# Prompt attention of a hybrid decoder layer: weighted values for two heads side by side with the values as the stationary operand, rows scaled before they are transposed, the causal term as a product

## The chip, the cores and the metric

The kernel runs on one core of a Trainium2 chip. The metric is the device time of one launch in microseconds (us); lower is better. Work on the core is spread over TensorE (PE for its matrix products, PEld for the loading of the stationary operand), VectorE (DVE), ScalarE (ACT), GpSimd (POOL) and SyncE (SP, which issues the transfers here). PE writes into eight PSUM banks of 128 partitions by 512 fp32 columns; DVE and ACT read these. A product of two fp32 operands is recorded as two passes, each with its own weight load; a transpose is recorded as one.

## What is computed

One layer of a decoder for a prompt (512 tokens) and eight short samples. The change touches one piece of it, the attention of the prompt over itself: 8 heads, keys 96 wide, values 64 wide, four blocks of 128 queries, softmax over the keys up to the query's own position.

```python
MLA_HEADS, MLA_V, SEQ, Q_BLOCK = 8, 64, 512, 128

def mla_scores(qn, qp, kn, kp):
    s = jnp.einsum('bthd,bshd->bhts', qn, kn) + jnp.einsum('bthd,bsd->bhts', qp, kp)
    return s.astype(jnp.float32) * MLA_SCALE

def mla_prompt_attention(qn, qp, kn, kp, v):
    ...
    def block(args):
        i, qn_i, qp_i = args
        s = mla_scores(qn_i, qp_i, kn, kp)
        qpos = i * qb + jnp.arange(qb)
        s = jnp.where(kpos[None, :] <= qpos[:, None], s, -jnp.inf)
        p = jax.nn.softmax(s, axis=-1).astype(v.dtype)
        return jnp.einsum('bhts,bshd->bthd', p, v)
    o = lax.map(block, (jnp.arange(nb), qn_b, qp_b))
    return o.swapaxes(0, 1).reshape(B, T, MLA_HEADS, MLA_V)
```

Its result, transposed, is one half of the input of the layer's output projection. Everything else of the layer (projections, a gated linear attention, the samples' attention over a paged cache, cross-attention, a squared-ReLU MLP) is the same in both kernels.

## The kernel before

The program is written as one instruction stream for each engine; the order on an engine is the order of the code, and engines meet only through semaphores. Phases end with `meet`, where every engine waits for the others. The prompt's attention lies between `meet(·, 2)` and `meet(·, 3)`. Its inputs are in SBUF by then: `qT` and `kT` (96 partitions, a head's queries and keys in columns), `vp` (values, tokens on partitions, 64 columns for each head).

The phase walks 32 steps `n`, one for each block of queries `t` (0 to 3) and head `h` (0 to 7). A step of block `t` looks at `t + 1` blocks of 128 keys, so its scores are 128 to 512 columns wide. For one step:

- PE, line 918: scores of 128 queries by (t+1)·128 keys, contraction over 96, into one of three banks (0, 1, 2 in turn).
- DVE, line 1874: adds the `causal` block (0 or a large negative number) to the last 128 columns, in the bank; line 1875: the negated maximum of each row.
- ACT, line 1419: exponential with that maximum as bias into `pr` (three buffers), and the row's sum into `stat`.
- PE, line 925: t+1 transposes of 128 by 128 of `pr` into bank 3 or 6.
- DVE (even steps, line 1881) or ACT (odd steps, line 1427): copy of these to `prT` (two buffers).
- PE, line 934: weighted values, t+1 products with a 128-column block of `prT` as the stationary operand and 64 columns of `vp` as the moving one, into columns 64h to 64h+64 of bank 4 or 5 (`po`). Queries are on partitions.

Once in a block, behind its eighth head: DVE takes reciprocals of the eight sums (line 1888) and scales all of `po` into `ot` (line 1891), PE transposes `ot` (line 911, four transposes) into bank 7, and ACT copies that to `mixT` (line 1433). The lag between the engines is written into the loops: PE's iteration `n` does the scores of step n, the transposes of step n-2 and the values of step n-3; ACT's iteration `n` does the exponential of step n and then, for odd n, the copy of step n-2.

`make_plan` gives each use of a bank its number; `full` waits for a bank's filling, `reopen` for its release. `link` makes an engine wait for its own last instruction. During the phase SP loads the pages of the first sample, and POOL prepares weights of the phase behind it.

## Time and profile before

| | |
|---|---|
| median of 3 runs | 1341.59 us (1338.92 to 1341.65) |
| the profiled execution | 1340.34 us, its span 1338.5 us |
| PE busy | 1265.8 us (95%), 7851 passes |
| PEld busy | 1085.6 us (81%) |
| DVE, ACT, POOL busy | 606.1, 380.6, 258.2 us |
| the prompt's attention | 339.5 to 404.5 us of the span |

The page divides the span into 40 slices and gives each engine's busy share in tenths; a row for the granted clock of TensorE stands below it. A matrix pass is recorded with its whole latency, so passes that follow each other overlap in the record, and PE can show as busy while it works at far less than its rate. How fast the passes really follow each other is read from their merged rows: n passes in a row take (n - 1) intervals and one latency. Idle time of PEld and PE in front of an instruction, with the engine that ended it, tells where PE truly stood.

### The profile page before, as it was taken

The numbers are of one execution on the slowest core, as the hardware profiler recorded it, in microseconds if no ns is written. First come the engines' busy times: TensorE is split into PE (matmuls) and PEld (weight loads), VectorE is DVE, ScalarE is ACT, GpSimd is POOL, SyncE is SP. The second block draws the span as 40 slices with busy tenths as digits, with TensorE's granted clock in tenths as the row PEclk, the third lists the DMA queues.
The fourth block names the chain that finished last, engine by engine and source line by source line (L and its number), as shares of the span: only waits on it lengthen the run. The fifth ranks groups of instructions, "written<-read, shape, count | busy, mean of one in ns | idle before, by whom it ended". The sixth has DMA issues, their size and how long they took to land.

```text
span 1338.5 us, 21880 instructions
## 1 busy us (share of the span) xinstructions
PE 1265.8 (95%) x7851; PEld 1085.6 (81%) x7851; DVE 606.1 (45%) x1025; ACT 380.6 (28%) x852; POOL 258.2 (19%) x150
## 2 busy tenths in 40 slices
PE   7999998888899999999998998799999999999997
PEld 4665677645779999999996776469999999999997
DVE  1213033597554666656663215254445444444343
ACT  5011002342444454444440125523331001331000
POOL 0201030220104665565652120011000000000000
PEclk9999999598799999999999998899999999999999
DMA  9511040020201122221210621213222222222201
GB/s 341 206 47 32 0 157 16 13 60 0 68 5 49 33 71 69 70 70 51 60 33 1 238 77 32 95 32 100 90 79 79 79 83 90 80 78 80 78 0 71
DMA packets 60834, 97.39 MB, mean 73 GB/s; under 512 B 22961, under 2 KB 39506, under 8 KB 60690
## 3 DMA queue, kind: packets, MB, share of 16 engines
q1 hardware_dynamic: 59906, 93.51, 22.5%
q0 software_dynamic: 848, 2.89, 0.7%
q8 instruction: 41, 0.67, 0.2%
q14 instruction: 39, 0.32, 0.1%
HBM read 91.12 MB, written 5.25 MB: 72 GB/s over the span
## 4 chain that ended last, share of the span: by engine, by line
PE 77%; DVE 11%; ACT 3%; issue 3%; POOL 3%; DMA 2%; POOLq 0%; DVEq 0%; SPq 0%; ACTq 0%
PE bank L1197 31%; PE bank L667 14%; PE bank L753 4%; PE bank L1025 3%; PE bank L1027 3%; POOL stat L2283 3%; PE bank L1026 3%; PE bank L691 2%; PE bank L977 2%; PE bank L1053 2%; PE bank L957 1%; PE bank L934 1%; PE bank L918 1%; DMA arena<-in_cache_mk_dram 1%; DVE stat L1917 1%
## 5 line engine op out<-in xcount | busy, mean ns | idle before, releaser
L1197 PE MATMUL bank<-ur,wr 128*128 128x288 f32 x1536 | 205.3, 296 | 0.0
L1197 PE MATMUL bank<-hr,wr 128*128 128x288 f32 x1536 | 205.3, 296 | 0.0
L1197 PEld LDWEIGHTS bank<-ur,wr 128*128 128x128 f32 x1536 | 205.0, 189 | 0.1
L1197 PEld LDWEIGHTS bank<-hr,wr 128*128 128x128 f32 x1536 | 204.9, 189 | 0.1
L2283 POOL TENSOR_TENSOR stat<-stat,cst 128x32 f32<-128x32 f32 x32 | 173.7, 5428 | 2.5
L1025 PE MATMUL bank<-wq_high,c_parts 128*128 128x288 f32 x512 | 162.5, 317 | 2.9 <-ACT hT L1451 2.4
L1027 PE MATMUL bank<-wq_low,c_parts 128*128 128x288 f32 x512 | 151.5, 296 | 0.0
L1026 PE MATMUL bank<-wq_high,c_parts 128*128 128x288 f32 x512 | 150.9, 295 | 0.0
L2106 DVE CAST wr<-ring 128x1024 fp32r<-128x1024 f32 x64 | 44.5, 695 | 208.7 <-PE bank L1197 207.9
L667 PE MATMUL bank<-hT,ring 128*128 128x288 f32 (+1 forms) x512 | 125.7, 407 | 0.0
L1917 DVE TENSOR_REDUCE stat<-hT 128x8 f32<-128x512 f32 x128 | 86.9, 683 | 78.9 <-ACT hT L1451 74.4
L667 PEld LDWEIGHTS bank<-hT,ring 128*128 128x128 f32 (+1 forms) x512 | 93.9, 184 | 30.4 <-issue 1.2
L1025 PEld LDWEIGHTS bank<-wq_high,c_parts 128*128 128x128 f32 x512 | 96.7, 189 | 7.8 <-ACT hT L1451 3.8
L1026 PEld LDWEIGHTS bank<-wq_high,c_parts 128*128 128x128 f32 x512 | 97.0, 189 | 0.0
L1027 PEld LDWEIGHTS bank<-wq_low,c_parts 128*128 128x128 f32 x512 | 96.5, 189 | 0.0
L1576 ACT ACTIVATE hT<-bank 128x288 f32<-128x288 f32 x32 | 13.2, 412 | 234.3 <-PE bank L1197 234.3
L2108 DVE TENSOR_TENSOR wr<-ring,wr 128x1024 fp32r<-128x1024 f32 x64 | 78.5, 1226 | 2.2
L1451 ACT ACTIVATE hT<-bank 128x512 f32<-128x512 f32 x128 | 77.9, 608 | 0.8 <-DVE stat L1917 0.2
L1443 ACT COPY arena<-bank 128x64 f32<-128x64 f32 x128 | 27.3, 213 | 140.7 <-PE bank L1027 98.7
L753 PE MATMUL bank<-ring,hT 128*128 128x512 f32 (+3 forms) x160 | 53.1, 488 | 0.0
L753 PEld LDWEIGHTS bank<-ring,hT 128*128 128x128 f32 (+1 forms) x160 | 28.2, 179 | 23.2 <-issue 20.5
L1908 DVE TENSOR_TENSOR c_parts<-bank,c_parts 128x512 fp32r<-128x512 f32 x64 | 43.7, 683 | 6.6 <-ACT c_parts L1459 6.5
(370 smaller groups left out, 1650.3 us busy)
## 6 DMA issues: line engine op xcount, KB each, us to landing
ring<-in_ring_w_dram SPq DMA_DIRECT2D x106, 512.0 KB, 3.6
arena<-in_cache_ckv_dram SPq DMA_DIRECT2D x128, 128.0 KB, 2.0
arena<-in_cache_mk_dram SPq DMA_DIRECT2D x8, 512.0 KB, 3.8
arena<-in_cache_mv_dram SPq DMA_DIRECT2D x8, 512.0 KB, 8.9
mixT<-in_x_dram SPq DMA_DIRECT2D x1, 2048.0 KB, 13.2
arena<-in_cache_kpe_dram SPq DMA_DIRECT2D x128, 16.0 KB, 1.6
out_dram<-hT SPq DMA_DIRECT2D x4, 512.0 KB, 2.6
mixT<-in_w_qb_dram SPq DMA_DIRECT2D x1, 1152.0 KB, 13.3
```

Source lines behind the costliest of these rows:

```text
L667: ins = mm(outs[c][0:m, 0:HALF], lhsT(k), src[:, k, c * HALF:(c + 1) * HALF], start=(k == 0), stop=(k == n_k - 1))
L753: ins = mm(o[0:m, 0:n_out], hTk[:, k, c0:c0 + m], ring[:, s0:s0 + n_out // P, k, :], start=(k == 0), stop=(k == KD - 1))
L1025: mm(o[:, 0:WQ - QH], c_parts[:, n % 2, 0, e, k, :], high, start=(k == 0), stop=False)
L1026: mm(o[:, 0:WQ - QH], c_parts[:, n % 2, 1, e, k, :], high, start=False, stop=False)
L1027: ins = mm(o[:, 0:WQ - QH], c_parts[:, n % 2, 0, e, k, :], low, start=False, stop=(k == KC - 1))
L1197: ins = mm(outs[c][:, 0:HALF], w[:, ew, k, :], src[:, ex, k0 + k, c * HALF:(c + 1) * HALF], start=(start and k == 0 and n == 0), stop=(sto ...
L1451: A(sqs[:, j % 2, :].rearrange("p (e c) -> p e c", e=2), o[:, :, keys_at:keys_at + WQ - 2 * QH], ACT.Square).then_inc(S("kr_free"), 1)
L1908: V.tensor_tensor(c_parts[:, n % 2, 1, :, :, :].rearrange("p e k c -> p (e k c)"), o[:, :], c_parts[:, n % 2, 0, :, :, :].rearrange("p e k ...
L1917: V.tensor_reduce(stat[:, 64 + 32 * g + 8 * (j % 4):72 + 32 * g + 8 * (j % 4)], sqs[:, j % 2, :].rearrange("p (h c) -> p h c", h=MH), AX.X ...
L2106: V.tensor_copy(wr[:, j % SPLITS, 0, :], src).then_inc(S("w_high"), 1)
L2108: V.tensor_tensor(wr[:, j % SPLITS, 1, :], src, wr[:, j % SPLITS, 0, :], ALU.subtract).then_inc(S("w_split"), 1)
L2283: G.tensor_tensor(r, r, power.broadcast_to([P, 32]), ALU.pow).then_inc(S("r_pg"), 1)
```

## The change

In the code of the phase:

- The causal block is no longer added by DVE. PE multiplies the identity with `causal` and accumulates it on the last 128 columns of the scores.
- DVE, behind the exponential of a step, takes the reciprocal of that step's row sums and scales the 128 rows of `pr` in place, before they are transposed. `pr` and `prT` have four buffers now.
- The weighted values are made for two heads at a time. The 64 columns of `vp` are the stationary operand and the 128-column block of `prT` the moving one; the result is transposed already (values on partitions, queries in columns), the even head on output partitions 0 to 63, the odd one on 64 to 127.
- So the scaling of `po`, the transposes of `ot` and bank 7 are gone, and ACT copies `po` itself to `mixT`.
- Lags: on PE the transposes are of step n-3 and the values of steps n-5 and n-4 (in iterations with odd n); ACT copies step n-3 ahead of its exponential of step n; DVE scales step n-1 in iteration n and copies step n-3.

```diff
@@ buffers @@
-        pr = view(hT, 0, 3, 512)
-        prT = view(hT, 1536, 2, 512)
-        ot = view(hT, 2560, 2, 512)
+        pr = view(hT, 0, 4, 512)
+        prT = view(hT, 2048, 4, 512)
@@ PE @@
-                    filled(mm(o[:, 0:(t + 1) * P], qT[0:MQ, h, t * P:(t + 1) * P], kT[0:MQ, h, 0:(t + 1) * P],
-                              start=True, stop=True), ("s", t, h))
-                if 2 <= n < len(steps) + 2:
-                    t, h = steps[n - 2]
-                    pe.wait_ge(S("pr"), n - 1)
+                    mm(o[:, 0:(t + 1) * P], qT[0:MQ, h, t * P:(t + 1) * P], kT[0:MQ, h, 0:(t + 1) * P],
+                       start=True, stop=False, skip_group_check=True)
+                    filled(mm(o[:, t * P:(t + 1) * P], ident, causal, start=False, stop=True, skip_group_check=True),
+                           ("s", t, h))
+                if 3 <= n < len(steps) + 3:
+                    t, h = steps[n - 3]
+                    pe.wait_ge(S("prn"), n - 2)
...
-                    for s in range(t + 1):
-                        ins = mm(o[:, h * MV:(h + 1) * MV], prT[:, (n - 3) % 2, s * P:(s + 1) * P],
-                                 vp[:, s, h * MV:(h + 1) * MV], start=(s == 0), stop=(s == t))
+                    for s in range(t + 1):
+                        for e in range(2):
+                            ins = mm(o[MV * e:MV * (e + 1), (h // 2) * P:(h // 2 + 1) * P],
+                                     vp[:, s, (h - 1 + e) * MV:(h + e) * MV], prT[:, (n - 5 + e) % 4, s * P:(s + 1) * P],
+                                     start=(s == 0), stop=(s == t))
...
-                if n >= 5 and steps[n - 5][1] == MH - 1:
-                    out_rows(steps[n - 5][0])
@@ ACT @@
+                if 3 <= n < len(steps) + 3 and (n - 3) % 2 == 1:
+                    t, h = steps[n - 3]
+                    o = full(act, ("pT", t, h))
+                    wait_prT_free(act, n - 3)
+                    nc.scalar.copy(prT[:, (n - 3) % 4, 0:(t + 1) * P], o[:, 0:(t + 1) * P]).then_inc(S("prT1"), 1)
...
-                    nc.scalar.copy(prT[:, 1, 0:(t + 1) * P], o[:, 0:(t + 1) * P]).then_inc(S("prT1"), 1)
...
-                    o = full(act, ("poT", t))
+                    o = full(act, ("po", t))
@@ DVE @@
-                    link(V.tensor_tensor(o[:, t * P:(t + 1) * P], o[:, t * P:(t + 1) * P], causal, ALU.add))
...
+                if 1 <= n < len(steps) + 1:
+                    t, h = steps[n - 1]
+                    dve.wait_ge(S("pr"), n)
+                    link(V.reciprocal(stat[:, 95 + n:96 + n], stat[:, 63 + n:64 + n]))
+                    row_n = pr[:, (n - 1) % 4, 0:(t + 1) * P]
+                    V.tensor_scalar(row_n, row_n, stat[:, 95 + n:96 + n], None, ALU.mult).then_inc(S("prn"), 1)
...
-                    link(V.reciprocal(stat[:, 0:8], stat[:, 64 + 8 * t:72 + 8 * t]))
-                    if t >= 2:
-                        full(dve, ("poT", t - 2))
-                    V.tensor_tensor(ot[:, t % 2, :].rearrange("p (h c) -> p h c", h=MH),
-                                    o[:, :].rearrange("p (h c) -> p h c", h=MH), spread(stat[:, 0:8], 2, MV),
-                                    ALU.mult).then_inc(S("ot"), 1)
```

What stands on PE in two steps of the last block, before (`cst` holds the identity; banks 0 to 2 take scores, 2/3 and 6 transposes, 4/5 the values; odd banks are printed under the even name of their pair):

```order
L918 MATMUL bank2<-arena 128x512
L925 MATMUL bank6<-cst,hT 128x128 x4
L934 MATMUL bank4<-arena,hT 128x64 x4
L918 MATMUL bank0<-arena 128x512
L925 MATMUL bank2<-cst,hT 128x128 x4
L934 MATMUL bank4<-arena,hT 128x64 x4
```

And with the change (L908 the scores, L910 identity by `causal`, L917 the transposes, L928 the values):

```order
L908 MATMUL bank0<-arena 128x512
L910 MATMUL bank0<-cst 128x128
L917 MATMUL bank6<-cst,hT 128x128 x4
L908 MATMUL bank2<-arena 128x512
L910 MATMUL bank2<-cst 128x128
L917 MATMUL bank2<-cst,hT 128x128 x4
L928 MATMUL bank4<-hT,arena 64x128 x8
```

Eight products for two heads stand behind every second step, where four for one head stood behind every step, and each score has a product of 128 columns more.

On DVE in the last block, before, with the semaphores that each instruction waits for:

```order
L1874 TENSOR_TENSOR bank2<-bank2,cst 128x128 [waits prT0,bank_full2]
L1875 TENSOR_REDUCE stat<-bank2 128x1 [waits dve_step]
L1874 TENSOR_TENSOR bank0<-bank0,cst 128x128 [waits bank_full0]
L1875 TENSOR_REDUCE stat<-bank0 128x1 [waits dve_step]
L1881 COPY hT<-bank2 128x512 [waits prT_used,bank_full3]
```

And with the change (L1867 the maximum, L1872 and L1874 reciprocal and scaling, L1879 the copy):

```order
L1867 TENSOR_REDUCE stat<-bank0 128x1 [waits prT0,bank_full1]
L1872 RECIPROCAL stat<-stat 128x1 [waits pr]
L1874 TENSOR_SCALAR hT<-hT,stat 128x512 [waits dve_step]
L1867 TENSOR_REDUCE stat<-bank2 128x1 [waits bank_full2]
L1872 RECIPROCAL stat<-stat 128x1 [waits pr]
L1874 TENSOR_SCALAR hT<-hT,stat 128x512 [waits dve_step]
L1879 COPY hT<-bank2 128x512 [waits bank_full4,bank_full3]
```

An instruction on 128 columns is gone from each step, and two are new, of which one runs over the step's whole width and waits for ACT's exponential.

On ACT, before and with the change:

```order
L1419 ACTIVATE hT,stat<-bank0,stat 128x512 [waits prT1,bank_full6,row_max]
L1419 ACTIVATE hT,stat<-bank0,stat 128x512 [waits pr,bank_full3,row_max]
L1427 COPY hT<-bank6 128x512 [waits pr,prT_used,bank_full6]
```

```order
L1419 ACTIVATE hT,stat<-bank0,stat 128x512 [waits prT1,bank_full3,row_max]
L1419 ACTIVATE hT,stat<-bank0,stat 128x512 [waits pr,bank_full6,row_max]
L1410 COPY hT<-bank6 128x512 [waits pr,prT_used,bank_full6]
```

The rows read alike, but the step numbers behind them moved: the copy before is of step n-2 and stands behind the exponential of step n, the copy now is of step n-3 and stands ahead of it.

## Rows read from the trace of the kernel before

**Rows 1.** Windows of the phase: us, busy (x count) by engine, PEclk, DMA share, GB/s.
```profile
339.50:344.00 4.50, 2.72 (x18) 2.11 (x18) 3.17 (x12) 2.25 (x10) 4.22 (x6) 1.00 0.26 71
344.00:361.00 17.00, 16.63 (x63) 13.68 (x63) 7.97 (x24) 6.90 (x26) 0.86 (x3) 0.50 0.38 108
361.00:397.20 36.20, 33.83 (x208) 24.94 (x207) 22.13 (x49) 17.34 (x45) 0.00 (x0) 1.00 0.05 8
397.20:404.50 7.30, 4.66 (x39) 4.05 (x37) 1.61 (x4) 2.54 (x5) 0.00 (x0) 1.00 0.00 0
```
**Rows 2.** Groups by line and form, 339.5 to 404.5: busy us, mean ns, idle before.
```profile
L934 PE MATMUL bank<-arena,hT 128*128 128x64 f32 x160 | 25.4, 294 | 4.5 <-ACT hT L1427 4.4
L925 PE MATMUL bank<-cst,hT 128*128 128x128 f32 x80 | 15.9, 298 | 0.9 <-ACT hT L1419 0.9
...
L1874 DVE TENSOR_TENSOR bank<-bank,cst 128x128 f32<-128x128 f32 x32 | 9.6, 299 | 23.3 <-PE bank L918 22.8
...
L1875 DVE TENSOR_REDUCE stat<-bank 128x1 f32<-128x512 f32 x8 | 5.5, 691 | 0.3
...
L1875 DVE TENSOR_REDUCE stat<-bank 128x1 f32<-128x128 f32 x8 | 2.3, 292 | 0.3
```
**Rows 3.** Waits of the phase: engine and line, for whom, us, times, longest.
```profile
ACT hT L1419 <- DVE stat L1875: 28.0, 29, 2.0
...
PEld bank L934 <- ACT hT L1427: 8.2, 13, 1.2
...
PEld bank L925 <- ACT hT L1419: 1.8, 4, 1.1
```
**Rows 4.** Timeline, one step of the last block: start us, us, engine, line.
```profile
392.56 1.08 PE L918 MATMUL bank<-arena 96*128 96x512 f32 x2
...
393.48 0.60 PE L925 MATMUL bank<-cst,hT 128*128 128x128 f32 x4
...
394.14 1.10 PE L934 MATMUL bank<-arena,hT 128*128 128x64 f32 x8
```
**Rows 5.** Timeline at the phase's start: PE waits for the first exponentials.
```profile
339.53 0.94 PE L918 MATMUL bank<-arena 96*128 96x128 f32 x6 [0.88 <-DVEq L456]
...
341.36 0.33 PE L925 MATMUL bank<-cst,hT 128*128 128x128 f32 x1 [0.90 <-ACT hT L1419]
```
**Rows 6.** Timeline at the phase's end.
```profile
400.24 1.94 PE L934 MATMUL bank<-arena,hT 128*128 128x64 f32 x16
...
402.45 0.69 DVE L1891 TENSOR_TENSOR hT<-bank,stat 128x512 f32<-128x512 f32 x1
403.20 0.66 PE L911 MATMUL bank<-cst,hT 128*128 128x128 f32 x4 [1.02 <-DVE hT L1891]
403.89 0.59 ACT L1433 COPY mixT<-bank 128x512 f32<-128x512 f32 x1 [2.87 <-PE bank L911]
```
**Rows 7.** Timeline, products elsewhere with 64-column stationary operands on alternate output halves.
```profile
462.60 3.69 PE L977 MATMUL bank<-arena 128*64 128x257 f32 x32 [0.16 <-ACT arena L1470]
...
735.36 1.20 PE L1077 MATMUL bank<-arena,w_kvb 128*64 128x64 f32 x32 [0.97 <-DVE arena L1974]
```
**Rows 8.** Timeline, PE going back from narrow to full-width stationary operands.
```profile
466.22 0.65 PE L978 MATMUL bank<-arena 64*64 64x257 f32 x2
466.79 0.19 PEld L1025 LDWEIGHTS bank<-wq_high,c_parts 128*128 128x128 f32 x1 [0.39 <-issue]
466.79 0.41 PE L1025 MATMUL bank<-wq_high,c_parts 128*128 128x288 f32 x1
```
**Rows 9.** Groups by line and form, whole span: scaling by a column, and a short reciprocal.
```profile
L1640 DVE TENSOR_SCALAR hT<-xT,gn 128x576 f32<-128x576 f32 x8 | 3.8, 514 | 0.1
L1630 DVE TENSOR_SCALAR arena<-cst,stat 128x128 f32<-128x128 f32 x4 | 0.9, 283 | 18.6 <-POOL stat L2186 18.6
L2065 DVE RECIPROCAL stat<-stat 128x2 f32<-128x2 f32 x8 | 1.3, 159 | 1.5 <-ACT arena L1523 1.5
```
**Rows 10.** Windows ahead of the phase, columns as in rows 1.
```profile
324.00:328.00 4.00, 2.07 (x14) 2.10 (x15) 3.58 (x5) 0.18 (x1) 0.00 (x0) 0.87 0.00 0
```

More of the change, by code:

```diff
@@ L167, in make_plan @@
         fill(("po", t), 4 + t % 2)
-        fill(("poT", t), 7)
     base = list(used)
@@ L489, in __call__, with wait_prT_free @@
                 self.eng.wait_ge(self.sem, self.n)
-        def wait_prT_free(eng, n, steps):
-            if n >= 2:
-                t, h = steps[n - 2]
-                if h < MH - 1:
-                    eng.wait_ge(S("prT_used"), (n - 2) - t)
+        def wait_prT_free(eng, n):
+            if n >= 4:
+                t, pair_h = (n - 4) // MH, (n - 4) % MH // 2
+                if pair_h < MH // 2 - 1:
+                    eng.wait_ge(S("prT_used"), (MH // 2 - 1) * t + pair_h + 1)
                 else:
@@ L904, in _ @@
             steps = [(t, h) for t in range(4) for h in range(MH)]
-            def out_rows(t):
-                pe.wait_ge(S("ot"), t + 1)
-                o = reopen(pe, ("poT", t))
-                for j in range(4):
-                    ins = tr(o[:, j * P:(j + 1) * P], ot[:, t % 2, j * P:(j + 1) * P], ident)
-                filled(ins, ("poT", t))
-            for n in range(len(steps) + 5):
+            for n in range(len(steps) + 4):
                 if n < len(steps):
@@ L933, in _ @@
                     for s in range(t + 1):
-                        ins = mm(o[:, h * MV:(h + 1) * MV], prT[:, (n - 3) % 2, s * P:(s + 1) * P],
-                                 vp[:, s, h * MV:(h + 1) * MV], start=(s == 0), stop=(s == t))
+                        for e in range(2):
+                            ins = mm(o[MV * e:MV * (e + 1), (h // 2) * P:(h // 2 + 1) * P],
+                                     vp[:, s, (h - 1 + e) * MV:(h + e) * MV], prT[:, (n - 5 + e) % 4, s * P:(s + 1) * P],
+                                     start=(s == 0), stop=(s == t))
                     if h < MH - 1:
@@ L1416, in _ @@
                     act.wait_ge(S("row_max"), n + 1)
-                    if n >= 3:
-                        full(act, ("pT", *steps[n - 3]))
-                    A(pr[:, n % 3, 0:(t + 1) * P], o[:, 0:(t + 1) * P], ACT.Exp, bias=stat[:, 32 + n:33 + n],
+                    if n >= 4:
+                        full(act, ("pT", *steps[n - 4]))
+                    A(pr[:, n % 4, 0:(t + 1) * P], o[:, 0:(t + 1) * P], ACT.Exp, bias=stat[:, 32 + n:33 + n],
                       accum_out=stat[:, 64 + n:65 + n]).then_inc(S("pr"), 1)
@@ L1422, in _ @@
                     act.nop().then_inc(bank_free[PLAN[("s", t, h)][0]], 1)
-                if 2 <= n < len(steps) + 2 and n % 2 == 1:
-                    t, h = steps[n - 2]
-                    o = full(act, ("pT", t, h))
-                    wait_prT_free(act, n - 2, steps)
-                    nc.scalar.copy(prT[:, 1, 0:(t + 1) * P], o[:, 0:(t + 1) * P]).then_inc(S("prT1"), 1)
-                    act.wait_ge(S("prT1"), (n - 2) // 2 + 1)
-                    act.nop().then_inc(bank_free[PLAN[("pT", t, h)][0]], 1)
                 if n >= 5 and steps[n - 5][1] == MH - 1:
                     t = steps[n - 5][0]
-                    o = full(act, ("poT", t))
+                    o = full(act, ("po", t))
                     freed(nc.scalar.copy(mixT[:, 4:8, t * P:(t + 1) * P], o[:, :].rearrange("p (j c) -> p j c", j=4)),
-                          ("poT", t))
+                          ("po", t))
             meet(act, 3)
@@ L1869, in _ @@
             steps = [(t, h) for t in range(4) for h in range(MH)]
-            for n in range(len(steps) + 5):
+            for n in range(len(steps) + 3):
                 if n < len(steps):
```

29 lines of the change are left out of this document (12 added, 17 removed).

## The prediction

> **What bounds the kernel now.** PE is busy for 95% of the span, so an edit counts if it shortens what PE does or waits for. The change lies wholly in the prompt's attention, 65 us of the span, and the phases on both sides meet all engines, so what this phase gains or loses is what the launch gains or loses. I read its windows first [rows 1], then its groups and waits [rows 2, 3], then single steps [rows 4 to 6], and last the rows of other phases that price what is new [rows 7 to 10].
>
> The windows show three things. From 344 to 361 us the clock is granted at half (1.2 of 2.4 GHz). PE records 16.63 of 17.00 us as busy there, so that stretch is work at half speed. Ahead of it, from 339.5 to 344, PE is busy for 2.72 of 4.5 us, waiting in between for the first exponentials [rows 5]. And the last 7.3 us hold only 4.66 us of PE.
>
> Next, work against waiting. Passes of 128 columns, or of 64 columns behind a full weight load, follow each other every 0.11 us at full clock (16 take 1.94 us and 8 take 1.10, so eight more take 0.84 [rows 4, 6]). Both passes of a 512-wide score take 0.92 us from their start to the transposes [rows 4]; I take 0.43 for one behind another, and 0.32, 0.21 and 0.11 for the narrower ones. In full-clock time the phase is: scores 8 x 2 x (0.11 + 0.21 + 0.32 + 0.43) = 17.1; transposes 80 x 0.11 = 8.8; values 160 x 0.11 = 17.6 [rows 2]; the transposes of line 911, 16 x 0.11 = 1.8. Sum 45.3. Half speed for 17 us adds 8.5: 53.8. From 339.5 to the last transposes at 403.9 there are 64.4 us, so 10.6 us are waits. They stand at the start (about 2.5), at the end (402.2 to 403.2 for the scaling, and 1.2 for the last copies), and for ACT's copies on the way: 8.2 us of PEld in 13 waits [rows 3]. That last is a loop: a score goes to DVE (mask, maximum), to ACT (exponential), and ACT's copy of an older step stands behind the exponential, while PE's values wait for the copy and the next score stands behind the values.
>
> **What the change does to PE's work.** Removed: line 911, 1.8, and the values' 17.6. Added: the causal product, 32 x 2 passes of 128 columns, 7.0. The values again: for two heads and t+1 key blocks there are 4(t+1) passes, as many as before. If the two halves of the array work side by side, they cost 2(t+1) intervals of 0.11: 80 x 0.11 = 8.8. Two phases do this now: 32 passes of 257 columns take 3.69 us, where one behind another at half the 512-wide price (0.215) would need 6.9; and 32 passes of 64 columns take 1.20 us, so that narrow weight loads keep up with 0.06 to 0.07 a pair [rows 7]. The change's 128 columns lie between these, so I take side by side.
>
> Against that stands the switch between full-width and 64-column operands, twice for each of 16 groups. In rows 8 the two narrow passes start at 466.22 and stream until about 466.65, and the full-width one starts at 466.79: 0.14 us at least. The weight loads show 0.39 us of idle there, at most what a switch costs. So 0.28 to 0.78 a group; I take 0.36, nearer to PE's own gap, since PE and not the loading sets the pace: 16 x 0.36 = 5.8 (4.5 to 12.5). The Trainium skill (TensorEngine Tiling, Key Properties) says that a change of the tiling mode drains TensorE, which speaks against this change. The gap in rows 8 agrees that there is a price.
>
> PE's new sum is 17.1 + 8.8 + 7.0 + 8.8 + 5.8 = 47.5, that is 2.2 us more than before at full clock. For two steps it is 1.7 us in block 0, then 2.5, 3.4 and 4.3. The gain can only come from waits and from the clock.
>
> **DVE and ACT.** For one step DVE loses the mask (0.30 [rows 2]) and gains a reciprocal (0.16) and the scaling: 0.28 us for 128 columns and 0.51 for 576 [rows 9], so 0.28, 0.35, 0.42 and 0.48. With the maximum (0.29 to 0.69 [rows 2]), half a copy as wide, and 0.05 of hand-over, a step costs DVE 0.95, 1.22, 1.5 and 1.76. PE needs 0.84, 1.27, 1.7 and 2.14. So DVE sets the pace in block 0, the two are level in block 1, and PE sets it in blocks 2 and 3. If scaling ran at twice its price, DVE would be at 2.2 in block 3, level with PE: no end of the range needs more. ACT does what it did. The causal product is hidden by nothing; the scaling is hidden behind PE from block 1 on. The wait of the transposes for the scaling has a lag of three steps, over 5 us in block 3 for a chain of 2.7 (score's end, maximum 0.7, reciprocal and scaling 0.7, latencies), so what is queued behind it on PE (the values and the next score) should not feel it. ACT's copy now stands ahead of the exponential, and the values follow it a step later: the loop of rows 3 is open.
>
> **The end.** Gone are the reciprocal, the scaling and the transposes between the last values and ACT's copy, 1.7 us between 402.2 and 403.9 [rows 6], beyond the 0.4 already counted. Late next are the last exponential, its scaling and transposes, and ACT's copy of them: PE waits some 0.7 us there.
>
> **The start and the clock.** Scores 0 to 2 with their causal products stand on PE until 340.9. The first exponential ends at about 341.2, as now [rows 5], the scaling at 341.7, and PE goes on with scores 3, 4 and 5 as their banks come free. DVE reaches its fourth maximum at about 342.5 and then needs 0.95 a step. Between 340.4 and 343.9 PE gets three scores with their products, the rest of the third and three transposes, about twice what it streams there now. The clock fell at 344, behind the waits of rows 5, and before the phase, behind another stretch in which PE stood half idle [rows 10]; it was full all through 361 to 397, where waits are short [rows 1]. So I expect that it does not fall in this phase. This is the choice on which most of the gain rests, and the rows can't prove it.
>
> **Sum.** With full clock: DVE's fourth step at 342.5, five at 0.95 and eight at 1.22 bring it to 357.1; PE is a step ahead, 356.0. There remain for PE 4 x (3.4 + 4.3) = 30.8 and the lagging transposes and values of block 1, 2.2: 389.0. With 0.7 for the last wait and 1.5 for waits that I don't see: 391.2. ACT's last copy, 0.65 with its hand-over, ends at 391.9, where the old one ends at 403.89 + 0.59 = 404.5. Gain 12.6 us. The profiled execution took 1340.34 us (its span is 1338.5), so it would take 1327.7; against the median of 1341.59, 1.25 us above it, **1329.0 us**.
>
> **Rivals.** (1) The clock falls at 344 as it does now, for 17 us. By 344 some 3.3 of the 47.5 are done (six scores with their products 2.6, three transposes, a first pair of values); 17 us do 8.5; 35.7 remain: 396.7, with 0.7 and 1.5 it is 398.9, and 399.6 with the copy. Gain 4.9: 1336.7 us. For it: the first wait is as long as now. Against: PE has no long wait behind it. (1b) It falls for part of that time, since PE has fewer gaps while it is slow: midway, 1332.9. (2) Switches cost what the weight loads show, 0.78 a group: 6.7 more, some of it under DVE in the first two blocks: gain 7, 1334.6. (3) The slower one: the halves don't work side by side on 128 columns in this order, where each product's two passes are on one half. Then 80 intervals more, 8.8 us. Alone it leaves a gain of 3.8 (1337.8). With the half clock of (1), where 24 of the 80 cost double, it is 8.8 + 2.6 - 4.9 = 6.5 us slower: 1348.1. It decides from 0.3 us a group on if the clock falls, and from 0.8 if not. Rows 7 speak against it. (4) That nothing changes since the time is hidden elsewhere is out: the phase ends in a meeting of all engines, and the next one starts behind it.
>
> **Chances.** The forecast 0.5; (1) 0.15; (1b) 0.15; (2) 0.1; (3) 0.07; the rest 0.03. The range goes from the forecast with no hidden waits and cheap switches (1.5 + 1.3 less, and 0.7 for the measurement) to (1): 1325.5 to 1337. It leaves out (3) and the tails. The measurement can tell about 0.2%, 2.7 us, from no change. Faster by more than that: 0.91; within it 0.04; slower 0.05.
>
> **What would show it.** Right: windows of the phase at 1.00; 52 to 53 us between its meetings; the values' passes in groups of 16 at about 1.0 to 1.3 us in block 3; PE's waits for ACT's copies gone; DVE without gaps in block 0, PE without gaps in blocks 2 and 3. Wrong: 0.50 in the windows (then (1)); groups of 16 at 1.8 us or more (3); idle of PEld ahead of each group and each score behind it of 0.3 us or more (2); PE waiting for the scaling, which would mean that DVE sets the pace in block 3 as well.

## The result, and the profile after

The changed kernel takes **1324.57 us** (median of 4 runs, 1323.39 to 1325.60) where the kernel before takes 1341.47 (4 runs, 1338.92 to 1341.65): a ratio of 0.9878, 95% interval 0.9861 to 0.9895, a gain of 16.9 us. In a later comparison the same pair gave 1327.70 and 1341.95, 0.9892 (0.9876 to 0.9908), a gain of 14.3 us. The prediction said 1329.0, in a range of 1325.5 to 1337.0. The sign held, and the phase's own gain (13.5 us, 12.6 forecast); the launch gained a third more than forecast (16.9 us, 12.6), and the time lies 0.9 us below the range.

| | before | after |
|---|---|---|
| the profiled execution (its span) | 1340.34 us (1338.5) | 1325.19 us (1323.4) |
| PE busy | 1265.8 us, 7851 passes | 1254.3 us, 7899 passes |
| mean granted clock | 0.961 | 0.969 |
| first score to first product of the next phase | 339.53 to 404.85 us, **65.3** | 339.50 to 391.31 us, **51.8** |
| first scores of steps 8, 16, 24, 31 | 347.90, 363.06, 378.61, 395.08 | 346.90, 356.26, 369.08, 382.72 |
| half clock in the phase | 344.0 to 361.1 us | none |
| half clock right behind it | 405.45 to 408.86 us | none |

Windows of the phase after, columns as in [rows 1]:

```profile
339.50:344.00 4.50, 3.59 (x25) 3.02 (x26) 3.27 (x10) 1.69 (x8) 4.24 (x6) 1.00 0.23 70
344.00:356.20 12.20, 11.86 (x91) 9.38 (x89) 10.60 (x42) 8.22 (x31) 0.82 (x3) 1.00 0.41 116
356.20:382.70 26.50, 26.50 (x190) 18.59 (x187) 20.13 (x53) 14.82 (x39) 0.00 (x0) 1.00 0.13 27
382.70:389.00 6.30, 5.62 (x54) 3.98 (x52) 4.22 (x10) 3.23 (x7) 0.00 (x0) 1.00 0.00 0
```

The second window is the one to compare: from 344 on, [rows 1] has 0.50 for 17 us, and here the clock stays at 1.00. In the third PE stands nowhere, 26.50 of 26.50 us. In the first it is busy for 3.59 us instead of 2.72.

Groups of the phase by line and form, 339.5 to 388.6, as in [rows 2] (L928 the values, L917 the transposes, L910 the causal product, L1874 the scaling):

```profile
L928 PE MATMUL bank<-hT,arena 128*64 128x128 f32 x144 | 11.2, 283 | 0.1
...
L910 PE MATMUL bank<-cst 128*128 128x128 f32 x64 | 12.3, 274 | 0.0
...
L1874 DVE TENSOR_SCALAR hT<-hT,stat 128x512 f32<-128x512 f32 x8 | 3.9, 486 | 0.3
L1874 DVE TENSOR_SCALAR hT<-hT,stat 128x128 f32<-128x128 f32 x8 | 3.6, 454 | 0.3
```

The values' idle time is 0.1 us where it was 4.5. The last line is odd: 128 columns take 454 ns on average and 512 columns 486; the prediction had 0.28 for 128. More on that below.

Waits of the phase, as in [rows 3]:

```profile
ACT hT L1410 <- PE bank L917: 12.8, 14, 1.9
DVE stat L1867 <- PE bank L910: 7.2, 15, 0.9
ACT hT L1419 <- DVE stat L1867: 6.7, 17, 1.9
...
PEld bank L928 <- issue: 2.3, 13, 0.3
```

The 8.2 us in which the values waited for ACT's copy are gone, and ACT waits 6.7 us for the maxima where it waited 28.0. ACT, DVE and the copies now wait for PE. The last line is the weight loads' idle time at the switches to 64-column operands.

PE in the last block, two steps and then the drain, as in [rows 4] (start us, us, engine, line):

```profile
382.72 1.02 PE L908 MATMUL bank<-arena 96*128 96x512 f32 x2
383.58 0.39 PE L910 MATMUL bank<-cst 128*128 128x128 f32 x2
383.80 0.60 PE L917 MATMUL bank<-cst,hT 128*128 128x128 f32 x4
384.33 1.09 PE L928 MATMUL bank<-hT,arena 128*64 128x128 f32 x16
385.36 1.36 PE L917 MATMUL bank<-cst,hT 128*128 128x128 f32 x8
```

Sixteen passes of values take 1.09 us. Less the 0.28 us of one pass that is 0.054 us from start to start, half of the 0.11 of full-width passes: the halves work side by side. And the end, as in [rows 6]:

```profile
388.50 0.58 ACT L1410 COPY hT<-bank 128x512 f32<-128x512 f32 x1 [1.86 <-PE bank L917]
389.23 1.09 PE L928 MATMUL bank<-hT,arena 128*64 128x128 f32 x16 [0.77 <-ACT hT L1410]
390.36 0.58 ACT L1426 COPY mixT<-bank 128x512 f32<-128x512 f32 x1 [1.28 <-PE bank L928]
```

### The profile page after: what moved, and what is told of

It reads as the page before. It is cut to its first block, busy times and chain, and to the rows that moved or that the text cites. A ratio compares the mean times of both kernels' runs of the same rounds, so it can differ in the third digit from the quotient of the medians.

```text
span 1323.4 us, 21987 instructions
## 1 busy us (share of the span) xinstructions
PE 1254.3 (95%) x7899; PEld 1074.7 (81%) x7899; DVE 609.3 (46%) x1049; ACT 380.1 (29%) x852; POOL 258.0 (19%) x150
## 4 chain that ended last, share of the span: by engine, by line
PE 79%; DVE 10%; POOL 3%; issue 3%; ACT 2%; DMA 2%; POOLq 0%; DVEq 0%; SPq 0%; ACTq 0%
PE bank L1190 31%; PE bank L665 14%; PE bank L751 4%; PE bank L1018 3%; PE bank L1020 3%; POOL stat L2269 3%; PE bank L1019 3%; PE bank L689 2%; PE bank L970 2%; PE bank L1046 2%; PE bank L908 1%; PE bank L950 1%; DVE stat L1903 1%; DMA arena<-in_cache_mk_dram 1%; PE bank L928 1%
## 5 line engine op out<-in xcount | busy, mean ns | idle before, releaser
L751 PEld LDWEIGHTS bank<-ring,hT 128*128 128x128 f32 (+1 forms) x160 | 28.3, 180 | 23.1 <-issue 20.5
```

What stands on the lines that cost most here:

```text
L751: ins = mm(o[0:m, 0:n_out], hTk[:, k, c0:c0 + m], ring[:, s0:s0 + n_out // P, k, :], start=(k == 0), stop=(k == KD - 1))
```

## Experiments

Three theories of what shortened the phase are compared. Theory A, on which the prediction put most of the gain: PE's clock no longer falls at the phase's start. Theory B: the values no longer wait for the loop score, maximum, exponential, copy, whatever the clock does. Theory C: the work itself got shorter (values side by side, DVE rid of the mask). The length of the phase in the profile, from the first score to the next phase's first product, is read beside the time of the launch. It is the sharper of the two: the changed kernel has 51.8 us in both of its profiles and the last kernel below 47.3 in both of its own, while their medians moved by 3.1 and 2.5 us between two comparisons. Behind the phase the two profiles of the changed kernel take 932.1 and 935.5 us, with 23.2 and 28.3 us of half clock there. Half of those 5.1 us, 2.6, is an estimate of what the clock has in these 3.5; no run separates it.

| kernel | phase us | half clock in it | right behind | median us (n) | ratio to before (95%) |
|---|---|---|---|---|---|
| before | 65.3 | 17.1 | 3.4 | 1341.47 (4) | |
| after | 51.8 | 0 | 0 | 1324.57 (4) | 0.9878 (0.9861 to 0.9895) |
| e1 mask on DVE | 57.0 | 17.1 | 0 | 1333.81 (5) | 0.9949 (0.9930 to 0.9967) |
| e2 product only | 60.3 | 0 | 3.4, from 0.6 ahead of the end on | 1336.63 (7) | 0.9960 (0.9942 to 0.9979) |
| e3 busy start | 61.5 | 0 | 3.4 | 1339.00 (10) | 0.9987 (0.9975 to 0.9999) |
| e4 full width | 56.3 | 0 | 0 | 1331.86 (4) | 0.9927 (0.9902 to 0.9952) |
| e5 POOL late | 50.5 | 0 | 0 | 1324.82 (5) | 0.9871 (0.9853 to 0.9888) |
| e6 lags only | 55.6 | 10.2 | 3.4, from 0.5 ahead of the end on | 1332.50 (4) | 0.9921 (0.9901 to 0.9942) |
| e7 idle start | 54.4 | 3.4 | 0 | 1327.64 (4) | 0.9886 (0.9868 to 0.9905) |
| e8 POOL late, one pass | 47.3 | 0 | 0 | 1324.76 (4) | 0.9870 (0.9853 to 0.9888) |
| e9 mask on DVE, busy | 54.7 | 0 | 0 | 1329.10 (4) | 0.9905 (0.9887 to 0.9923) |
| e10 lags, busy | 52.5 | 0 | 6.8, from 0.9 ahead of the end on | 1328.89 (4) | 0.9910 (0.9891 to 0.9930) |
| e11 after again | 51.8 | 0 | 0 | 1327.70 (5) | 0.9892 (0.9876 to 0.9908) |
| e12 as e8, again | 47.3 | 0 | 0 | 1322.22 (4) | 0.9854 (0.9835 to 0.9873) |

The kernel before took 1341.56 beside e1 to e4, 1342.82 beside e5 to e8, and 1341.95 beside e9 to e12. The median of a kernel is compared with that of the kernel before beside it; across the groups only the phases are compared.

### e1: the changed kernel, with the causal term back on DVE

```diff
-  mm(o[:, t*P:(t+1)*P], ident, causal, start=False, stop=True)                            # PE
+  link(V.tensor_tensor(o[:, t*P:(t+1)*P], o[:, t*P:(t+1)*P], causal, ALU.add))           # DVE
```

> The changed kernel with one part undone: the causal block is added by DVE in the bank, as before, and PE has no product for it. PE loses 7.0 us of work at full clock, DVE gains 32 additions of 0.30 us with a hand-over of 0.04. My theory (DVE sets the pace in blocks 0 and 1 already, 0.95 and 1.22 us a step, and would be level with PE in block 3): the steps of blocks 0 and 1 get 0.34 us longer each, 16 x 0.34 = 5.4 us, block 2 about 1 us in all, block 3 nothing, so 1330 to 1332 us; the clock stays full or falls for a while in the first block, since PE has less to do, which would add up to 4 us. Rival (the product's 7 us on PE are what counts): 1318 to 1320 us.

Measured: 1333.81 us; the phase is 5.2 us longer than after. The windows, columns as in [rows 1]:

```profile
339.50:343.80 4.30, 2.27 (x14) 1.69 (x14) 3.52 (x12) 1.38 (x6) 4.05 (x6) 1.00 0.23 66
343.80:360.90 17.10, 16.35 (x62) 10.57 (x60) 13.44 (x54) 8.33 (x30) 0.95 (x3) 0.50 0.35 109
360.90:396.30 35.40, 31.25 (x232) 18.98 (x230) 29.23 (x82) 19.10 (x49) 0.18 (x2) 1.00 0.05 8
```

The clock falls at 343.80, as before, behind a start in which PE is busy for 2.27 of 4.3 us. In the last row DVE is busy for 29.23 of 35.40 us and PE no longer without a gap: with the mask on it, DVE is close to the limit in the last blocks too. But the loss is not there: counted from the phase's start, step 16 starts 5.5 us later than in the changed kernel (22.2 against 16.8 us) and step 24 is 4.8 later (34.4 against 29.6). So 5.2 us hold two causes in blocks 0 and 1, half clock and DVE's time, which e9 parts.

### e2: the kernel before, with the product alone

```diff
-  link(V.tensor_tensor(o[:, t*P:(t+1)*P], o[:, t*P:(t+1)*P], causal, ALU.add))           # DVE
+  mm(o[:, t*P:(t+1)*P], ident, causal, start=False, stop=True)                            # PE
```

> The kernel before with one part of the change: the causal block as a product on PE, nothing else. Theory (what mattered at the start is that PE streams more while it waits for the first exponentials, so the clock does not fall at 344): the windows from 344 on show 1.00, 8.5 us of half speed go, 7.0 us of PE work come at full clock, the chain from score to exponential is 0.34 us shorter for DVE and 0.22 longer for PE: 1333 to 1337 us. Rival (the clock falls as before): PE has 7.0 us more, of which a part at half speed, and saves on waits: 1341 to 1346 us.

Measured: 1336.63 us, the phase 60.3. As expected: 5.0 us of the phase's 13.5 come with a product that adds 7.0 us of passes to PE. The first two windows:

```profile
340.50:345.00 4.50, 3.83 (x29) 3.41 (x30) 1.98 (x8) 2.44 (x11) 4.12 (x6) 1.00 0.20 62
345.00:361.00 16.00, 14.75 (x103) 12.74 (x102) 6.64 (x19) 8.58 (x31) 0.95 (x3) 1.00 0.39 116
```

PE is busier at the start, and the clock stays at 1.00 where it fell before.

### e3: the kernel before, with PE kept busy at the start by products that nobody reads

```diff
+  if 2 <= n < 9:                                   # PE, ahead of the transposes
+      for _ in range(4 if n == 2 else 1):
+          mm(bank[7][:, 0:P], ident, ident, start=True, stop=True)
```

> The kernel before with nothing changed but ten products of the identity with itself (128 columns, two passes each, 2.2 us at full clock) put on PE in the first nine iterations, four of them where it waits for the first exponential; they write to a bank that nobody reads then. They are extra work. Theory (the clock fell because PE stood still for too much of the start): the clock stays full through the phase, and 8.5 us less what then waits on the loop through ACT, about 2, is saved: 1334 to 1336 us. Rival (the clock does not depend on what PE does there, or it matters little): 1341.5 to 1344 us.

Measured: 1339.00 us, 3 us above what was expected; the phase 61.5. The clock held, so the edit does what it should:

```profile
337.60:342.00 4.40, 3.73 (x28) 3.31 (x29) 3.17 (x12) 2.11 (x10) 4.08 (x6) 1.00 0.20 63
342.00:361.00 19.00, 15.41 (x102) 12.60 (x103) 11.52 (x34) 9.58 (x33) 1.01 (x3) 1.00 0.35 101
361.00:399.00 38.00, 33.35 (x212) 24.96 (x211) 20.21 (x44) 17.33 (x42) 0.06 (x2) 1.00 0.04 6
```

But 17 us of full clock bring only 3.8 us in the phase, not 8.5, and less in the launch (2.6, and the interval just leaves out no change). The ten products themselves are 2.2 us of passes; if none of that were hidden in PE's waits, full clock would be worth 6.0, still under 8.5. In the second window PE has 3.6 us of gaps at full clock, where [rows 1] shows 16.63 of 17.00 us as busy at half: the faster PE waits for the loop through ACT. As the whole explanation, theory A falls here.

### e4: the changed kernel with full-width values

```diff
-  mm(o[MV*e:MV*(e+1), cols], vp[:, s, (h-1+e)*MV:(h+e)*MV], prT_of_e, start=(s == 0), stop=(s == t))
+  mm(o[:, cols], vp[:, s, (h-1)*MV:(h+1)*MV], prT_of_e, start=(s == 0 and e == 0), stop=(s == t and e == 1))
```

Both heads' 128 columns of values are the stationary operand, so no mode is switched and nothing runs side by side; the separation of the two heads is left out.

> The changed kernel, but the values of both heads are one stationary operand of 128 columns, and each head's weights are streamed against both; so there is no switch to narrow operands and nothing goes side by side. It leaves out the separation of the two heads (their results are added up in the same columns); passes and bytes are as many. Theory (side by side saves 0.11 us for each of 2(t+1) intervals, a switch costs 0.15): in blocks 2 and 3, where PE sets the pace, 56 intervals more, 6.2 us, less 8 x 0.3 = 2.4 for the switches: about 3.8 us slower than the changed kernel, and up to 1 more from block 1: 1328 to 1330 us. Rival (the narrow passes don't go side by side, or a drain eats it): 1320 to 1325 us.

Measured: 1331.86 us, above the 1328 to 1330 expected; the phase 4.5 us longer than after, where about 3.8 and up to 1 more was expected, clock 1.00 throughout. Twelve passes of values, in e4 and in the changed kernel:

```profile
372.57 1.50 PE L928 MATMUL bank<-hT,arena 128*128 128x128 f32 x12
```
```profile
376.03 0.88 PE L928 MATMUL bank<-hT,arena 128*64 128x128 f32 x12
```

The intervals are 0.111 and 0.055 us: two halves side by side save 8.8 us of passes in all. In blocks 0 and 1 next to nothing of that counts: step 16 starts 16.9 us into the phase in e4 and 16.8 in the changed kernel. The switch is therefore priced where PE is busy throughout. Scores two steps apart start at 378.18 and 383.01 in e4, and at 376.84 and 381.10 in the changed kernel: 4.83 and 4.26 us. Sixteen passes at 0.055 instead of 0.111 save 0.90 and 0.57 are left, so a switch costs 0.33 a group. The same sum gives 0.35 in block 2 (3.73 and 3.40 us, twelve passes).

### e5: the changed kernel, with POOL's preparation of the next phase's weights behind the scalings of blocks 0 and 1

```diff
+  pool.wait_ge(S("prn"), 16)                       # POOL, ahead of wq_high and wq_low
```

> The changed kernel, but POOL starts the preparation of the next phase's weights only behind the sixteenth scaled step instead of at the phase's start. Theory (in the changed kernel the first three scalings of 128 columns took 0.70, 1.04 and 0.46 us, and each ended 0.08 us behind a POOL instruction that was running when it began; the later ones took 0.29: DVE and POOL exclude each other): the first three come down to 0.29, PE's start of the phase with them, 1.0 to 1.3 us less, and in block 2 DVE has slack to take the same waits: 1323.3 to 1323.8 against 1324.6. Rival (the long ones come from the loading of the pages or from the first use): no change, 1324.6.

Measured: the phase 50.5, 1.3 us shorter than after, as expected, and all of it ahead of step 16 (15.4 us into the phase instead of 16.8). The launch, 1324.82 us, doesn't show it: it was expected at 1323.3 to 1323.8 and can't be told from the changed kernel. The rows of DVE are in the last section.

### e6: the kernel before, with the lags and buffers of the changed one alone

```diff
-  pr = view(hT, 0, 3, 512);  prT = view(hT, 1536, 2, 512)
+  pr = view(hT, 0, 4, 512);  prT = view(hT, 2048, 4, 512)
   PE:  transposes of step n-2 -> n-3, values of step n-3 -> n-4
   ACT: copy of step n-2 behind the exponential of n -> copy of n-3 ahead of it
   DVE: copy of step n-2 -> n-3;  end of a block one iteration later
```

Mask, values and the scaling of whole blocks stay as before.

> The kernel before with only the lags and buffers of the change: four buffers for the weights and their transposes, transposes of step n-3, values of step n-4, ACT's copy ahead of the exponential. Mask on DVE, values one head at a time, scaling at the block's end, all as before. Theory (the loop from score through exponential and ACT's copy back to the values cost some 4 us in blocks 2 and 3, and the clock falls as before, since the start is as empty or emptier): the copies' waits of 8.2 us go, PE sets the pace: 3 to 5 us less than before, 1336.5 to 1338.5. Rival (the waits only move, to the transposes or to DVE): 1340 to 1342.

Measured: 1332.50 us, the phase 55.6. The gain in the phase is 9.8 us, two to three times what was expected of it, and the largest of any single part. The edit changes three things at once, the lags, the order on ACT and the buffers; which of them counts was not tried. The windows:

```profile
339.50:343.60 4.10, 2.71 (x17) 2.05 (x17) 2.99 (x13) 2.07 (x9) 3.70 (x5) 1.00 0.24 64
343.60:353.80 10.20, 10.20 (x40) 8.69 (x38) 5.83 (x20) 4.91 (x20) 1.37 (x4) 0.50 0.40 117
353.80:395.00 41.20, 39.48 (x268) 31.54 (x266) 26.20 (x59) 21.74 (x56) 0.00 (x0) 1.00 0.10 24
```

The clock falls at the same place. But PE has no gap while it is at half (10.20 of 10.20 us), and full clock is back 7 us earlier; behind that PE has 1.7 us of gaps in 41.2. Theory B carries most of the phase's gain, and part of A's effect (7 us less of half clock) comes with it.

### e7: the changed kernel with an idle PE at the start

```diff
+  for k in range(6):                               # DVE, ahead of its first maximum
+      V.tensor_reduce(stat[:, 620+k:621+k], cst[:, 0:512], AX.X, ALU.max)
```

> The changed kernel with six reductions of 512 columns put on DVE ahead of its first maximum, about 4 us in which PE has nothing to do after three scores. It is extra work. Theory (the clock falls behind such a wait, and then PE is at half speed for 7 to 17 us): 4 us of delay and 3.5 to 8.5 us of half speed: 1332 to 1337; in the windows 0.50 from about 344. If PE's fewer gaps bring the clock back sooner than in the kernel before, the stretch is shorter than 17 us. Rival (the clock does not follow PE's wait): 1328.7.

Measured: 1327.64 us, where 1332 to 1337 was expected: a miss. The phase is 54.4, 2.6 us longer than after. The timeline and the windows:

```profile
341.10 3.65 DVE L1863 TENSOR_REDUCE stat<-cst 128x1 f32<-128x512 f32 x6
...
345.60 0.49 PE L908 MATMUL bank<-arena 96*128 96x128 f32 x2 [2.94 <-ACTq L1422]
```
```profile
341.00:346.00 5.00, 2.00 (x15) 1.81 (x16) 4.47 (x11) 0.83 (x4) 4.63 (x7) 1.00 0.26 79
346.00:349.50 3.50, 3.50 (x19) 2.84 (x19) 2.84 (x15) 2.19 (x10) 0.46 (x1) 0.51 0.34 104
349.50:353.00 3.50, 3.50 (x28) 2.87 (x28) 2.45 (x12) 1.87 (x8) 0.00 (x0) 1.00 0.51 126
```

PE stood for 2.94 us and the clock did fall, at 346.03. But behind it PE was busy without a gap, and the clock was full again at 349.44. Here a fall cost the changed kernel 2.6 us in the phase, the gap ahead of it included; rivals (1) and (1b) put it at 8 and 4.

### e9 and e10: mask on DVE, and lags only, each with the products of e3

```diff
+  if 2 <= n < 9: ...  mm(bank[7][:, 0:P], ident, ident, ...)     # as in e3, into e1 and into e6
```

> The kernel of e1 (the change without the causal product; its clock fell from 344 to 361) with the ten extra products of e3 on PE in the first nine iterations. Theory (the causal product is worth its hold on the clock and the 0.34 us a step that it takes off DVE in blocks 0 and 1): the clock stays full; since DVE sets the pace in e1 at about 1.28 us a step in block 0 and 1.6 in block 1, of the 8.5 us of half speed only 2 to 4 come back: the phase takes 53 to 55 us instead of e1's 57.0, against 51.8 with the change: 1329.5 to 1331.5 us. Rival (the clock's whole price comes back, the product is worth nothing else): phase 49 us, 1325.

> The kernel of e6 (the kernel before with the change's lags alone; phase of 55.6 us, clock at half for 10.2 us of it) with the ten extra products of e3. Theory (with open loops and full clock PE sets the pace; its work is 45.3 us and the extra 2.2, so the pairing, the scaling and the product buy nothing beyond that): the phase takes 49.5 to 51.5 us, as long as with the whole change, 51.8, and the launch 1325 to 1328 us. Rival (the pairing of heads is worth several us of its own): phase 54 us or more, 1330.

Measured, e9: 1329.10 us, the phase 54.7, clock held. The product's 5.2 us in the changed kernel are therefore some 2.3 for the clock (57.0 to 54.7, with the extra products' own cost in it) and 2.9 for DVE's time (54.7 to 51.8; 2.4 of it stand ahead of step 16). e10: 1328.89 us, the phase 52.5, 0.7 us above the changed kernel and a little longer than the 49.5 to 51.5 expected. Its windows:

```profile
339.00:344.00 5.00, 4.70 (x37) 4.27 (x38) 3.82 (x16) 2.58 (x12) 4.50 (x7) 1.00 0.25 73
344.00:361.00 17.00, 16.75 (x109) 13.45 (x108) 13.49 (x38) 11.12 (x37) 0.57 (x2) 1.00 0.37 106
361.00:390.70 29.70, 28.68 (x199) 22.91 (x197) 17.73 (x37) 14.44 (x36) 0.00 (x0) 1.00 0.06 9
```

With lags and held clock alone, PE is busy nearly throughout, and the phase is within 0.7 us of the changed kernel's. That 0.7 is a balance. Counted from the phase's start, e10 begins step 16 at 15.5 us and step 24 at 27.9, the changed kernel at 16.8 and 29.6; from there to the end e10 takes 24.6 us and the changed kernel 22.2. So the change loses 1.3 us up to step 16, as much as POOL's work costs it there (e5), and gains 2.4 in block 3 and at the end. And e10 holds its clock by products that nobody reads; with the kernel's own work alone (e6) the phase is 3.8 us longer than the changed kernel's.

### e11, e8 and e12: the changed kernel again, and POOL late with the product in one pass

```diff
+  nc.scalar.copy(c_parts[:, 1, 1, 0, 0, :], ident)          # ACT, ahead of the phase, to fp32r
+  nc.scalar.copy(c_parts[:, 1, 1, 0, 1, :], causal)
-  mm(o[:, t*P:(t+1)*P], ident, causal, ...)
+  mm(o[:, t*P:(t+1)*P], c_parts[:, 1, 1, 0, 0, :], c_parts[:, 1, 1, 0, 1, :], ...)
```

> The changed kernel once more, unchanged, for more executions of it and of the kernel before on one chip. The phase gained 13.5 us in the first pair of profiles, the medians differ by 16.9. Theory (the rest is where the clock's half-speed stretches happen to fall elsewhere, 1.7 us for each, and a few samples): a mean granted clock of 0.968 to 0.970 against 0.961 to 0.963, and a difference of 14 to 17 us between medians. Rival (the change saves something outside the phase in every execution): over 17.

> The kernel of e5 with the identity and the causal block as fp32r copies, made by ACT ahead of the phase, so that the causal product is one pass instead of two. Theory (a pass costs 0.11 us where PE sets the pace, in blocks 2 and 3, and nothing in blocks 0 and 1): 16 x 0.11 = 1.8 us less than e5: 1321.5 to 1322. If the one pass is half as long too, up to 0.8 more. Rival (another engine limits there): as e5.

> The kernel of e8 once more, beside the changed kernel on the same chip. In e8 the phase took 47.3 us against 51.8, but the mean granted clock was 0.967 against 0.9695, so the medians were level. Theory (the phase's 4.5 us are real, the clock elsewhere varies from execution to execution): 2 to 5 us faster than e11. Rival (what the phase gains is given back at the clock elsewhere each time): level with e11 within 1 us.

Measured, e11: 1327.70 us and 14.3 us gained with a mean clock of 0.969, as expected. e8 and e12: the phase 47.3 us in both, 3.2 less than e5, where 1.8 and up to 0.8 more was expected. Scores two steps apart in block 3 start at 373.62 and 377.56 in e8 and at 376.09 and 380.35 in e5: 3.94 and 4.26 us, so 0.16 a pass. Blocks 2 and 3 give 2.5 us of the 3.2, and block 1, where nothing was expected, the other 0.7. Windows of e12:

```profile
344.00:353.80 9.80, 9.33 (x70) 7.01 (x69) 8.69 (x34) 7.21 (x26) 0.00 (x0) 1.00 0.38 110
353.80:377.90 24.10, 24.10 (x174) 16.20 (x172) 20.56 (x53) 14.88 (x40) 5.22 (x8) 1.00 0.18 40
```

The launch of e8 took 1324.76 us, no less than e5 beside it and 3 us above what was expected, with a mean clock of 0.9667 over its executions where e5 had 0.9694. Over 1322 us that difference is 3.6 us of clock, an estimate that would cover the 3.2; that it does so isn't shown. e12, the same kernel, took 1322.22, beside 1327.70 for the changed kernel (e11) in the same comparison, with 0.9692: 5.5 us less, where 2 to 5 was expected. It is the fastest kernel of the study.

## Why the prediction was right in kind and too high

Two steps of the prediction failed: that the launch gains exactly what the phase gains, and the term of 1.5 us for waits that were not seen. The rest of the miss comes from how medians lie to the profiled execution, for which the range had too little room.

**What bounds the kernel: half right.** The phase was the place to look, its clock and its loop were the two causes, and full clock for the whole phase was the choice that came true. But the split of the old phase was wrong. The forecast came near in spite of it, since its sum is built from PE's and DVE's steps at full clock and doesn't use the split; the rivals (1) and (1b) do take its 8.5 us over. Half speed was booked at 8.5 us and the waits at 10.6. The runs give, for the phase:

| | loop closed (old lags) | loop open (new lags) |
|---|---|---|
| clock falls | 65.3 (before) | 55.6 (e6) |
| clock held by extra products | 61.5 (e3) | 52.5 (e10) |

The clock is worth 3.8 or 3.1 us (up to 2.2 more, if the extra products' own passes are nowhere hidden), the lags 9.8 or, with the products in both kernels, 9.0. A PE that reads as busy at half clock (16.63 of 17.00 us [rows 1]) was taken for a PE that sets the pace. e3 shows that it didn't: at full clock the same stretch fills with gaps.

**PE's work: right.** Two steps were put at 3.4 us in block 2 and 4.3 in block 3; scores two steps apart start at 362.29 and 365.69, and at 376.84 and 381.10, so 3.40 and 4.26. The side-by-side price (8 pairs 0.87 us) held, and rival (3) with it fell (e4). The switch was put at 0.36 a group. In the rows above the last transpose starts at 384.13, 0.20 us ahead of the first value, and the last value 0.21 us ahead of the next transpose, where 0.11 is the normal interval; so these two places have 0.2 us, and e4 against the changed kernel gives 0.33 for a whole group. Rival (2), 0.78, is out. The Trainium skill (TensorEngine Tiling, Key Properties) says that a change of tiling mode drains TensorE: these rows agree that it costs. But the first value starts 0.20 us behind a transpose that is recorded for 0.27, so in these records PE does not stand until that one has ended.

**DVE and ACT: right from block 1 on, wrong at the start.** The scaling of 512 columns took 486 ns (0.48). In block 0 the first three took 0.70, 1.04 and 0.46 instead of 0.28, and the fourth maximum began at 343.37, where 342.5 was forecast. The first score of step 16 was still at 356.26 against 356.0, since the later steps took a little less than estimated. e5 prices the omission at 1.3 us.

**The end: right, with an addition that wasn't there.** The last wait is 0.77 us (0.7), the chain of reciprocal, scaling and transposes is gone. ACT's last copy ends at 390.94 us, where 391.9 was forecast. The step that failed here is the 1.5 us "for waits that I don't see": PE has none from 356.2 to 382.7, as the third window of the changed kernel shows. Without it the sum would have given 390.4, 0.5 us early: 0.3 of that stands at step 16 already, and the last wait has 0.1.

**The step that failed outright: "what this phase gains or loses is what the launch gains or loses".** In the profiled pair 15.15 us were gained: 13.5 in the phase and 1.6 outside it, for which the prediction had no term. One difference outside is seen in the rows. Right behind the phase the kernel before ran 3.4 us at half clock, with its sparse end in front (4.66 of 7.3 us [rows 1]). The window behind the meeting, before and then after:

```profile
404.80:409.00 4.20, 4.15 (x21) 3.85 (x22) 1.54 (x4) 1.76 (x3) 0.00 (x0) 0.59 0.10 16
```
```profile
391.30:396.00 4.70, 4.02 (x31) 3.80 (x32) 1.51 (x4) 1.84 (x5) 0.00 (x0) 1.00 0.07 11
```

All five kernels with the old end (before, e2, e3, e6, e10) have such a stretch from the end of the phase on; none of the nine profiles with the new end has one. At half of its 3.4 us it is worth 1.7, an estimate, and the mean length of the next phase is 1.7 us more in the five (395.5 us from its first product to that of the phase behind it, 393.8 in the nine). But other stretches of half clock come and go: the nine lie between 392.0 and 395.3. In the profiled pair the next phase gained 0.8 us (394.4 to 393.6) and the rest of the launch another 0.8; and in the second profile of the changed kernel, from the later comparison, all that lies outside the phase takes 1274.5 us, more than the 1273.2 before. So a gain outside the phase is likely on the mean of the profiles, and for one pair it is not shown where it comes from.

**The range.** From the forecast of 1329.0 to 1324.57 there are 4.4 us: 0.9 in the phase, 1.6 outside it, and 1.9 because the median before lay 1.25 us above its profiled execution while the median after lies 0.6 below its own. The lower end allowed 2.8 us for the first and 0.7 for the last, and nothing for the second. 0.7 was too little by what stood ahead of the prediction already: three runs of one kernel were 2.7 us apart. In the second comparison the gain was 14.3 us, inside the range (whose lower end stands for 16.1) and near the phase's 13.5. So by how much the forecast was too high depends on the executions drawn; the 0.9 us in the phase doesn't.

**The chances.** The forecast's case came. Rivals (1) and (1b) had 0.3 between them, at 8 and 4 us; e7 shows a fall in the changed kernel that costs 2.6 us in all: PE had no gap behind it, and its clock was full again after 3.4 us, not 17. The rivals took the 17 us from a kernel with a closed loop. That the clock would hold was argued from PE's fuller start, without a row that could prove it; e1 bears it out, which fell at 343.8 with 2.27 us of PE in the first 4.3, where the changed kernel has 3.59 in 4.5.

What stays open: which of the second-order parts (pairing of heads, scaling by row, product) pay for which, given the lags. Together they are worth 0.7 us in the phase against the lags with a clock held by extra products (e10), and 3.8 against the lags alone (e6). e1 and e4 show that, within the whole, taking one away costs 4.5 to 5.2. A reading that fits is that each pays for what another adds (the product for the scaling on DVE, the two halves for the product on PE); no run takes two of them away.

## What to carry to other kernels

Where PE runs at half clock and reads as busy, don't book half of that time as gain: a few extra products that hold the clock up tell what full clock is worth (here 3.8 us for 17, less than half), and whether a loop through other engines takes its place. Look for that loop first: one more step of lag for transposes and values, the copy ahead of the exponential and four buffers gave 9.8 of 13.5 us without a change to any instruction's work. And count the phase behind: with the sparse end it began at half clock in all five kernels. Last, judge an edit of one phase by that phase's length in the profile: in two kernels it repeated to 0.1 us, while their medians moved by 3.1 and 2.5.

## What the runs showed of the hardware

**DVE's scaling waits for POOL.** DVE (L1867 maximum, L1872 reciprocal, L1874 scaling) and POOL at the start of the changed kernel's phase:

```profile
341.41 0.70 DVE L1874 TENSOR_SCALAR hT<-hT,stat 128x128 f32<-128x128 f32 x1
342.03 0.28 DVE L1867 TENSOR_REDUCE stat<-bank 128x1 f32<-128x128 f32 x1
342.23 0.15 DVE L1872 RECIPROCAL stat<-stat 128x1 f32<-128x1 f32 x1
342.41 1.04 DVE L1874 TENSOR_SCALAR hT<-hT,stat 128x128 f32<-128x128 f32 x1
```
```profile
340.21 1.26 POOL L2245 TENSOR_TENSOR wq_low<-w_kvb,wq_high 128x512 fp32r<-128x512 f32 x1
341.43 0.60 POOL L2244 CAST wq_high<-w_kvb 128x512 fp32r<-128x512 f32 x1
342.11 1.26 POOL L2245 TENSOR_TENSOR wq_low<-w_kvb,wq_high 128x512 fp32r<-128x512 f32 x1
```

Both scalings start while a POOL instruction runs (341.41 under one that ends at 341.47, with the next right behind it; 342.41 under one that ends at 343.37), and both end 0.08 us behind POOL's (342.11 and 342.03; 343.45 and 343.37), while maximum and reciprocal between them keep their usual time. In e5, where POOL does this work later, the same instruction takes 0.29:

```profile
341.97 0.29 DVE L1874 TENSOR_SCALAR hT<-hT,stat 128x128 f32<-128x128 f32 x1
342.17 0.28 DVE L1867 TENSOR_REDUCE stat<-bank 128x1 f32<-128x128 f32 x1
342.37 0.15 DVE L1872 RECIPROCAL stat<-stat 128x1 f32<-128x1 f32 x1
342.56 0.29 DVE L1874 TENSOR_SCALAR hT<-hT,stat 128x128 f32<-128x128 f32 x1
```

The Trainium skill (SBUF — State Buffer, Who interferes with whom) says that DVE's two-port mode, which a tensor_scalar on SBUF can enter, and GpSimd lock each other out of a shared port pair for a whole instruction. These rows agree in that DVE waits each time; none shows POOL waiting. The prediction should have asked what POOL does under each new instruction of DVE.

**The clock comes back at different speeds.** It fell at the start of the phase in four kernels, each behind gaps of PE, and stayed at half for 17.1 us before and in e1, 10.2 in e6 and 3.4 in e7. While it was at half, PE was recorded as busy for 16.63 of 17.00 us before, 16.35 of 17.10 in e1, 10.20 of 10.20 in e6 and 3.50 of 3.50 in e7: the two kernels without a gap in that stretch had it back sooner. What sets the difference between their 10.2 and 3.4 us is open.
